# Making the tables of further tiles four steps earlier in two expert layers, and loading expert 29's down weights into X instead of ROW

## The chip, the cores and the metric

The kernel runs on one core of one Trainium2 chip. The metric is the device time of one execution in microseconds (us), as the median of several runs. The five engines are TensorE (PE, with PEld for its weight loads), VectorE (DVE), ScalarE (ACT), GpSimd (POOL) and SyncE (SP). SP computes nothing here: it only issues transfers, in program order, each behind the waits that its buffer needs.

## The reference

Two transformer blocks over 256 tokens of width 1024 in float32. Block one has latent attention beside a long convolution, cross attention and a mixture of 32 experts; then comes a root-mean-square norm. Block two has a recurrent layer beside block attention, and again 32 experts. What matters here is the expert layer, and the norm between the blocks:

```python
for g in range(N_GROUPS):                       # block one: 4 groups of 8 experts
    a = jnp.einsum('td,edf->tef', t, w_gate[g])
    b = jnp.einsum('td,edf->tef', t, w_up[g])
    m = jax.nn.silu(a) * b * combine[:, g, :, None]
    y = y + jnp.einsum('tef,efd->td', m, w_down[g])
...
return _rms(x, final_norm_g)                    # between the blocks
...
hdn = jax.nn.silu(jnp.einsum('td,edf->tef', xc, w1)) * jnp.einsum('td,edf->tef', xc, w3)
return jnp.einsum('tef,efd->td', hdn * gate[:, :, None].astype(hdn.dtype), w2)   # block two
```

`combine` and `gate` are zero but for two experts of each token.

## The kernel before

**Experts.** `moe(b)` handles block b (1 or 2) on each engine. The 512 pairs of token and expert are sorted by expert, and each expert has one *tile* of slots: 32 slots in block one, 64 in block two. The layer is a row of 32 *steps*, one for each expert. In step e TensorE does gate and up of expert e (L1253 in block one, L1248 in block two), adds the rows of expert e-2 to the tokens (L1296), and does the down product of expert e-1 (L1268). VectorE in its step e does `hidden(e-1)`, `x_window(e+1)`, `to_slots(e-1)` and `low_part(e-1)`; the last one ends in L2829 and L2835 in block two.

**Further tiles.** An expert with more pairs than slots needs further tiles, which are run after the 32 steps. Their number, start, expert and rank come from tables on one partition, which VectorE makes piece by piece inside four of its steps: `extra_counts`, `extra_slots`, `extra_starts`, `extra_experts`. The last one writes the results as integers to `tabi` and raises the semaphore `routed`. The variable `looped` fixes the four steps: they are `looped - 4` to `looped - 1`, which is 12 to 15 in block one and 8 to 11 in block two. Steps below `looped` are written out, and those from `looped` to 27 run in a hardware loop. In block one the tables lie in the tile X, in block two in XN. In block two `order_of_steps`, at step 2, also writes the order in which experts 8 to 30 are taken.

**Weights.** Each expert has 2 MB of gate and up weights and 1 MB of down weights. SP issues them as two transfers. Block one has six places for them: four in `ring`, and two beside it, whose down halves are the tiles ROW and HT (`apart`). Expert 6's down weights go to X once. `in_six` refills a place as soon as `gu_done1` or `down_done1` say that its last user is through; the down weights of expert e wait for expert e-6's down product. Expert 29's go to ROW. Block two has the four places of `ring`, and one outside for expert 4. There expert e's weights wait for expert e-4's products (from expert 9 on). Experts 5 to 11 are issued by written-out code (L704, L706). Then SP waits until `routed` is 3 (L708), which is what `extra_experts` of block two raises it to, and issues experts 12 to 31 in a loop (L714, L716).

**Between the blocks.** ROW also takes `final_norm_g`, spread over all partitions by a transfer of 0.5 MB that POOL issues (L3352) when `down_done1` says that 30 down products are through. `gained` on VectorE (L3050, L3052) needs it. From it follow the norm of block two, TensorE's transposes of it (L783), the products `ada(10)` and `ada(11)` with two 2 MB pieces of `w_ada` (L924), and the input projection `xl` (from L798). `ada11` can be issued only when the last down product of block one has freed its place.

Of the kernel before, what the change touches and what calls it, by code (L numbers as in the profile page):

```python
# [46 lines left out]
NE = G * EPG  # L47
# [8 lines left out]
RING = 4  # L56
SLOT = 3 * KD * FE
# [114 lines left out]
SIX = RING + 2  # L172
# [3 lines left out]

GU = 2 * KD * FE
FEAT = S + 2 * FFN


STAGES = [("f1", 1, (1,)), ("hT", 4, (6, 7, 2, 4)), ("lat", 2, (3, 0)), ("f2", 1, (5,)), ("f3_0", 4, (1, 6, 7, 2)),
# [90 lines left out]
def two_blocks(nc, A, out):  # L272

    ctx = ExitStack()
    with ctx:
# [5 lines left out]
        def sem(name):  # L281
            if name not in made:
                made[name] = ctx.enter_context(nc.semaphore(name))
            return made[name]
# [4 lines left out]
        X = sb("X", [P, TT, D])  # L289
# [303 lines left out]
        def _(sp):  # L593
# [4 lines left out]
            def in_six(w):  # L598

                base = MOE_AT[0]  # L600

                def refill_gate(e, q, src):

                    s = slot(base + q)
                    sp.wait_ge(sem("gu_done1"), e - (SIX - 1))
                    if q < RING:
                        sp.dma_start(ring[:, s, 0:GU], src[:, 0:GU]).then_inc(sem(f"slot_full{s}"), 16)
                    else:
                        sp.dma_start(apart[q - RING][0], src[:, 0:GU]).then_inc(sem(f"beside_gu{q - RING}"), 16)

                def refill_down(e, q, src, places=SIX):

                    sp.wait_ge(sem("down_done1"), e - (places - 1))
                    if q < RING:
                        sp.dma_start(ring[:, slot(base + q), GU:SLOT], src[:, GU:SLOT]).then_inc(sem(f"slot_down{q}"), 16)
                    else:
                        sp.dma_start(apart[q - RING][1], src[:, GU:SLOT]).then_inc(sem(f"beside_d{q - RING}"), 16)

                refill_gate(SIX, 0, w[SIX, :, :])
                for e in range(SIX + 1, 2 * SIX + 1):  # L620
                    refill_gate(e, e % SIX, w[e, :, :])
                    refill_down(e, (e - 1) % SIX, w[e, :, :], SIX + 1)
                with sp.Fori(2 * SIX + 1, NE - 2 * SIX, SIX) as e0:
                    for q in range(SIX):
                        src = w[bass.ds(e0 + q, 1)].rearrange("a p f -> p (a f)")
                        refill_gate(e0 + q, (q + 1) % SIX, src)
                        refill_down(e0 + q, q, src)
                for e in range(NE - SIX - 1, NE - 1):
                    refill_gate(e, e % SIX, w[e, :, :])
                    if e == NE - 2:  # L630
                        refill_gate(NE - 1, (NE - 1) % SIX, w[NE - 1, :, :])
                    refill_down(e, (e - 1) % SIX, w[e, :, :])
                refill_down(NE - 1, (NE - 2) % SIX, w[NE - 1, :, :])

            def half_outside(w, q):
# [97 lines left out]

            at = dict(UNITS)["filt"] - FEAT
            for t in range(TT):
                sp.dma_start(X[:, t, :], A["x"][t * P:(t + 1) * P, :]).then_inc(sem(f"x_in{t}"), 16)
            sp.dma_start(tab[:, 0:P], A["tab"][:, 0:P]).then_inc(sem("tab"), 16)
            sp.dma_start(col[:, :], A["col"]).then_inc(sem("tab"), 16)
            sp.dma_start(ring[:, slot(0), at:at + FEAT], A["filt"][:, at:at + FEAT]).then_inc(sem("feat"), 16)
            load(PLACE["lat"], A["lat"], dict(UNITS)["lat"])  # L740
# [10 lines left out]
            n = experts(0)  # L751
# [14 lines left out]
        def _(pe):  # L766
# [202 lines left out]
            w = arrived(pe, "mla")  # L969
# [141 lines left out]
            def moe(b):  # L1111
# [8 lines left out]
                for k in range(KD):  # L1120
                    ready(pe, f"rT{b}", k // 2)
                    g = 64 * (k % 2)
                    n = min(64, KD * (G + NE) - k * (G + NE))
# [186 lines left out]
                    return (r - ways) % RING if in_turn(e) else r  # L1310

                uses_1 = [-(-(NE - q) // SIX) for q in range(SIX)]
                downs_1 = [-(-(NE - 1 - q) // SIX) for q in range(SIX)]

                def gate_of_six(n, r):

# [7 lines left out]

                def down_of_six(n, r):

                    if r == SIX and isinstance(n, int):
                        pe.wait_ge(sem("down_in_x"), 16)
                        return X[:, :, :].rearrange("p t d -> p (t d)")
                    if r > SIX or not isinstance(n, int):  # L1330
                        r = r - 1
                    q, use = r % SIX, r // SIX
                    if q >= RING:
                        pe.wait_ge(sem(f"beside_d{q - RING}"), n * 16 + 16 * (use + 1))
                        return apart[q - RING][1]
                    pe.wait_ge(sem(f"slot_down{q}"), n * 16 + 16 * (use + 1))
                    return ring[:, slot(base + q), GU:SLOT]
# [111 lines left out]
                looped = NE - RING  # L1449
# [19 lines left out]
                n = pe.value_load(tabi[0:1, XCOUNT[b]:XCOUNT[b] + 1], min_val=0, max_val=NX[b] - 1)  # L1469
# [4 lines left out]
                with pe.If(n > 0):  # L1474
                    with pe.Fori(0, n) as j:
                        w = ring[:, slot(base + 4 - 2 * b), :]
# [727 lines left out]
        def _(dve):  # L2204
# [367 lines left out]
            for h in range(XH):  # L2572
                ready(dve, f"xs{h}")
                link(V.reciprocal(xinv[:, h, :], xsum[:, h, :]))
                for t in range(TT):
                    p = prob[:, h % 2, t, :]
# [37 lines left out]
            def moe(b):  # L2614
# [241 lines left out]
                r = slice(0, 1)  # L2856
                c1, s1, x1, xi1, xe1 = counts[r, :], starts[r, :], nx[r, :], xincl[r, :], xex[r, :]
                mk, tm, mb = mk8[b][r], tm8[b][r], mk8b[b][r]
                n = NX[b]
# [67 lines left out]
                if b == 1:  # L2927
# [5 lines left out]
                    dve.wait_ge(sem("silu1"), 2)  # L2933
                    dve.wait_ge(sem("down_done1"), 1)
                    times_up(hb).then_inc(sem("hb1"), 1)
                looped = (5 - b) * RING
                for e in range(3 - b, looped):
                    if b == 1 and e == 2:
                        x_window(3, 1)
# [385 lines left out]
        def _(pool):  # L3325
# [56 lines left out]
            pool.dma_start(relb[0:BUCKETS, :], A["rel_bias_2"]).then_inc(sem("onehot"), 16)  # L3382
            G_.memset(relb[BUCKETS:BUCKETS + 1, :], NEG).then_inc(sem("mask_row"), 1)
            pool.wait_ge(sem("mask_row"), 1)
            pool.wait_ge(sem("down_done1"), SIX * (NE // SIX))
            broadcast_row(ROW[:, 0:1024], "final_norm_g", D, "rows")
            pool.wait_ge(sem("f_gain"), 2 * TT)
            pool.dma_start(ROW[:, 0:1024], A["gates_w"]).then_inc(sem("gates_w"), 16)
# [99 lines left out]
```

## Time and profile before

| | us |
|---|---|
| median of 3 runs | 922.76 |
| the runs | 922.76, 1696.45, 921.23 |
| profiled execution, device time | 919.3 |
| its span, first to last instruction | 917.4 |
| TensorE busy in it | 857.7 |
| VectorE busy in it | 532.2 |
| ScalarE busy in it | 362.2 |

The 1696.45 stands alone and belongs to a disturbed run. The profiled execution took 919.3, of which 917.4 is the span and 1.9 lies around it; all times of rows count from the start of the span. Block one's steps lie between about 306 and 505 us, block two's between about 665 and 904 us. The whole span moved 285.39 MB at a mean of 311 GB/s, and its chain of waits is put down to TensorE for 62%, to transfers for 17% and to VectorE for 12%. A busy share is an average over stages with different limits, so the rows of one stage say more than these.

### The profile page before, as it was taken

To read this page: it belongs to the slowest core of one execution; us is meant where nothing else is said; L and a number is where in the kernel's file an instruction comes from. 1 tells how busy PE (TensorE), PEld (TensorE's weight loads), DVE (VectorE), ACT (ScalarE), POOL (GpSimd) and SP (SyncE) were. 2 spreads that over 40 slices of the span, in tenths; PEclk is the share of its full clock that TensorE was granted. 3 is DMA by queue.
4 is the path that set the end of the run, shared out by engine and by line. 5 is a ranking of instruction groups with operands and counts; after the bars stand their busy time and mean duration, and the time that the engine had idled before them with its cause. 6 is when DMAs were issued, how large, how long until landed. Compare 5 with 4: busy or idle time off the path is not lost.

```text
span 917.4 us, 15466 instructions
## 1 busy us (share of the span) xinstructions
PE 857.7 (93%) x5774; PEld 543.9 (59%) x5774; DVE 532.2 (58%) x1182; ACT 362.2 (39%) x711; POOL 22.3 (2%) x41
## 2 busy tenths in 40 slices
PE   8999999999999899989998799999899979999995
PEld 6778558888976333433433499766654535555552
DVE  5877668465455645675554775988843543333335
ACT  5574435455354333323332657645421111111113
POOL 1010111000000000000000000000000000000000
PEclk9999999999999999999999999999999989999998
DMA  9655895547647899999999985613789849999991
GB/s 353 252 192 222 321 386 201 186 167 270 265 165 309 345 411 424 424 425 427 424 426 420 422 315 200 233 44 121 292 304 384 321 196 429 425 422 424 426 420 50
DMA packets 28904, 285.39 MB, mean 311 GB/s; under 512 B 3080, under 2 KB 5544, under 8 KB 7856
## 3 DMA queue, kind: packets, MB, share of 16 engines
q1 hardware_dynamic: 25344, 278.25, 75.1%
q0 software_dynamic: 1136, 3.74, 1.2%
q10 hardware_dynamic: 2368, 2.64, 0.9%
q8 instruction: 36, 0.59, 0.3%
q14 instruction: 20, 0.16, 0.0%
HBM read 283.56 MB, written 1.06 MB: 310 GB/s over the span
## 4 chain that ended last, share of the span: by engine, by line
PE 62%; DMA 17%; DVE 12%; ACT 4%; issue 3%; SPq 1%; DVEq 1%; ACTq 0%
DMA ring<-in_experts 14%; PE bank L798 8%; PE bank L1248 7%; PE bank L800 7%; PE bank L799 7%; PE bank L1268 6%; PE bank L1253 4%; PE bank L1296 4%; PE bank L1219 3%; DVE ring_r L535 2%; PE bank L1260 2%; DMA ring<-in_ada 2%; PE bank L924 1%; PE bank L1225 1%; DMA ring<-in_lat 1%
## 5 line engine op out<-in xcount | busy, mean ns | idle before, releaser
L535 DVE TENSOR_TENSOR ring_r<-ring,ring_r 128x1024 fp32r<-128x1024 f32 (+1 forms) x84 | 99.4, 1213 | 66.8 <-ACT ring_r L528 66.7
L1248 PE MATMUL bank<-ring,arena 128*64 128x256 f32 x992 | 115.7, 386 | 12.8 <-DMA ring<-in_experts 12.2
L528 ACT ACTIVATE ring_r<-ring 128x1024 fp32r<-128x1024 f32 (+1 forms) x84 | 85.0, 1046 | 68.5 <-PE bank L800 67.6
L798 PE MATMUL bank<-HT_r,ring_r 128*128 128x256 f32 x352 | 101.9, 289 | 1.3 <-DVE arena_r L2269 0.7
L1248 PEld LDWEIGHTS bank<-ring,arena 128*64 128x64 f32 x992 | 75.0, 138 | 45.9 <-issue 13.2
L800 PE MATMUL bank<-HT_r,ring_r 128*128 128x256 f32 x352 | 99.6, 283 | 0.0
L1268 PE MATMUL bank<-ring,arena 128*64 128x512 f32 (+1 forms) x416 | 81.7, 600 | 1.6 <-DMA ring<-in_experts 1.0
L799 PE MATMUL bank<-XN_r,ring_r 128*128 128x256 f32 x288 | 81.5, 283 | 0.0
L2829 DVE SCALAR_TENSOR_TENSOR arena<-bank,arena 128x512 f32<-128x512 f32 x32 | 24.0, 750 | 99.0 <-PE bank L1268 99.0
L1962 ACT ACTIVATE arena<-bank 128x512 f32<-128x512 f32 (+1 forms) x64 | 31.4, 491 | 117.5 <-PE bank L1248 94.8
L1296 PE MATMUL bank<-arena_r 64*128 64x512 f32 x496 | 74.2, 417 | 2.9 <-DVE arena_r L2836 2.4
L798 PEld LDWEIGHTS bank<-HT_r,ring_r 128*128 128x128 f32 x352 | 67.4, 192 | 4.5 <-issue 4.3
L1296 PEld LDWEIGHTS bank<-arena_r 64*128 64x128 f32 x496 | 41.8, 184 | 47.1 <-issue 33.3
L800 PEld LDWEIGHTS bank<-HT_r,ring_r 128*128 128x128 f32 x352 | 67.5, 192 | 0.0
L1977 ACT ACTIVATE arena_r<-arena 128x512 fp32r<-128x512 f32 x31 | 19.5, 630 | 103.7 <-DVE arena L2829 103.7
L799 PEld LDWEIGHTS bank<-XN_r,ring_r 128*128 128x128 f32 x288 | 55.2, 192 | 1.0 <-issue 1.0
L2836 DVE SCALAR_TENSOR_TENSOR arena_r<-bank,arena,arena_r 128x512 fp32r<-128x512 f32 x31 | 23.3, 751 | 51.6 <-ACT arena_r L1976 51.6
L1260 PEld LDWEIGHTS bank<-tab,arena 128*128 128x128 f32 x192 | 19.9, 140 | 51.0 <-issue 50.3
L1253 PE MATMUL bank<-ring,arena 128*32 128x512 f32 x352 | 42.3, 598 | 4.4 <-DMA ring<-in_experts 2.1
L1268 PEld LDWEIGHTS bank<-ring,arena 128*64 128x64 f32 (+1 forms) x416 | 20.4, 125 | 43.2 <-issue 40.3
L798 PE MATMUL bank<-ring_r,HT_r 128*128 128x512 f32 (+1 forms) x96 | 37.6, 391 | 1.7 <-DVE ring_r L535 1.3
L800 PE MATMUL bank<-ring_r,arena_r 128*128 128x512 f32 x96 | 37.6, 391 | 0.0
(509 smaller groups left out, 1439.1 us busy)
## 6 DMA issues: line engine op xcount, KB each, us to landing
ring<-in_experts SPq DMA_DIRECT2D x53, 2048.0 KB, 19.1
ring<-in_experts SPq DMA_DIRECT2D x52, 1024.0 KB, 16.5
ring<-in_ada SPq DMA_DIRECT2D x12, 2048.0 KB, 11.5
arena<-in_experts SPq DMA_DIRECT2D x10, 2048.0 KB, 17.8
ring<-in_win SPq DMA_DIRECT2D x5, 2048.0 KB, 14.9
ring<-in_hy SPq DMA_DIRECT2D x3, 2048.0 KB, 17.2
HT<-in_experts SPq DMA_DIRECT2D x6, 1024.0 KB, 15.2
ROW<-in_experts SPq DMA_DIRECT2D x5, 1024.0 KB, 15.7
```

Of the source, the lines that this page charges most:

```text
L528: nc.scalar.activation(R(h), w, ACT.Copy).then_inc(sem("w_high"), 1)
L535: nc.vector.tensor_tensor(R(w), w, R(h), ALU.subtract).then_inc(sem("w_low"), 1)
L798: mm(ps, R(ah), R(bh), start=first, stop=False)
L799: mm(ps, R(ah), R(bl), start=False, stop=False)
L800: return mm(ps, R(al), R(bh), start=False, stop=last_)
L1219: last = mm(list_bank[g:g + wide, :], picked[:, i, t, :], XN[:, t, h * 512:(h + 1) * 512], start=True, stop=True)
L1248: last = mm(gu_bank[g * wide:(g + 1) * wide, 0:256], xw[:, k, :], w[k // 4][:, k % 4, g * 256:(g + 1) * 256], start=k == 0, stop=k == KD - 1)
L1253: last = mm(gu_bank[g:g + wide, :], xw[:, 2 * (k % 4) + k // 4, :], w[k // 4][:, k % 4, :], start=k < sides, stop=k >= KD - sides)
L1260: last = tr(guT_bank[:, c * P:(c + 1) * P], gu_sb[:, c * P:(c + 1) * P], ident)
L1268: last = mm(d_bank[g:g + wide, :], hb[:, f, :], w[:, o:o + 512], start=b == 1 or f == 0, stop=b == 1 or f == 1)
L1296: last = mm(acc[2 * t + h][:, :], R(onto[b][rows, i, t * P:(t + 1) * P]), R(u[rows, :]), start=False, stop=False)
L1962: A_(gu_sb[:, 0:gu_cols], gu_bank[:, 0:gu_cols], ACT.Copy).then_inc(sem(f"gu_sb{b}"), 1)
```

## The change

`looped` is 4 lower for both blocks. Block one's tables are made in steps 8 to 11, block two's in steps 4 to 7, and VectorE's hardware loops begin at 12 and 8. Expert 29's down weights go to X, behind two waits: `routed` at 1 (block one's tables, which lie in X, are finished) and `down_done1` at 7 (expert 6's down weights, which lie there too, are used). With that ROW's last user is expert 23, and POOL may issue the `final_norm_g` transfer when `down_done1` is 24. The rest counts the semaphores anew. No instruction is added or dropped in what is executed.

```diff
+DOWN_IN_X = (SIX, NE - 3)
...
-                    refill_down(e, (e - 1) % SIX, w[e, :, :])
+                    if e == DOWN_IN_X[1]:
+                        sp.wait_ge(sem("routed"), 1)
+                        sp.wait_ge(sem("down_done1"), SIX + 1)
+                        sp.dma_start(X[:, :, :].rearrange("p t d -> p (t d)"), w[e, :, GU:SLOT]).then_inc(sem("down_in_x"), 16)
+                    else:
+                        refill_down(e, (e - 1) % SIX, w[e, :, :])
...
-                downs_1 = [-(-(NE - 1 - q) // SIX) for q in range(SIX)]
+                downs_1 = [-(-(NE - 1 - q) // SIX) - (q == (DOWN_IN_X[1] - 1) % SIX) for q in range(SIX)]
...
-                    if r == SIX and isinstance(n, int):
-                        pe.wait_ge(sem("down_in_x"), 16)
+                    if isinstance(n, int) and r in DOWN_IN_X:
+                        pe.wait_ge(sem("down_in_x"), 16 * DOWN_IN_X.index(r) + 16)
                         return X[:, :, :].rearrange("p t d -> p (t d)")
...
-                looped = (5 - b) * RING
+                looped = (4 - b) * RING
...
-            pool.wait_ge(sem("down_done1"), SIX * (NE // SIX))
+            pool.wait_ge(sem("down_done1"), DOWN_IN_X[1] - SIX + 1)
             broadcast_row(ROW[:, 0:1024], "final_norm_g", D, "rows")
```

On VectorE, at step 7 of block two, before the change (from `hidden(6)` to `to_slots(6)`; `waits` names the semaphores, and TENSOR_LOAD reads a number of `tabi`):

```order
L2775 TENSOR_TENSOR arena<-arena,bank 128x128 [waits down_done2,silu2]
L2611 TENSOR_LOAD tabi
L2611 ISA x2
L2815 ISA [waits gu_done2]
L2815 COPY arena<-arena 128x512
L2822 COPY arena<-arena 128x2 [waits to_tokens2]
L2825 TENSOR_SCALAR arena_r<-tab,arena 128x256 [waits cur2]
```

The same place after the change (line numbers are 6 higher here):

```order
L2821 COPY arena<-arena 128x512
L2925 TENSOR_TENSOR XN<-XN,tab 1x256
L2926 TENSOR_REDUCE XN<-XN 1x8 [waits dve_step]
L2927 CAST tabi<-XN 1x8 [waits dve_step]
L2928 CAST tabi<-XN 1x8
L2929 CAST tabi<-XN 1x8
L2930 CAST tabi<-arena 1x1
L2960 TENSOR_LOAD tabi [waits routed]
L2960 ISA x2
L2962 TENSOR_LOAD tabi
L2962 ISA x2
```

The last piece of block two's tables, with the CAST that raises `routed`, stood at step 11 and stands at step 7 now, between the copy of the next expert's tokens and `to_slots(6)`.

On SP, at expert 29 of block one, before:

```order
L609 DMA arena<-in_experts 128x4096 [waits gu_done1]
L617 DMA ROW<-in_experts 128x2048 [waits down_done1]
L607 DMA ring<-in_experts 128x4096 [waits gu_done1] x2
L617 DMA HT<-in_experts 128x2048 [waits down_done1]
L615 DMA ring<-in_experts 128x2048 [waits down_done1]
```

and after:

```order
L610 DMA arena<-in_experts 128x4096 [waits gu_done1]
L636 DMA X<-in_experts 128x2048 [waits down_done1,routed]
L608 DMA ring<-in_experts 128x4096 [waits gu_done1] x2
L618 DMA HT<-in_experts 128x2048 [waits down_done1]
L616 DMA ring<-in_experts 128x2048 [waits down_done1]
```

The transfer keeps its place in SP's order; its destination and the counts that it waits for are others.

## Rows read from the trace of the kernel before

**Rows 1.** The profile's page: the span.
```profile
span 917.4 us, 15466 instructions
```
**Rows 2.** Waits of SP's queue: us in total, times, longest.
```profile
SPq L708 <- DVE tabi L2924: 17.5, 1, 17.5
```
**Rows 3.** Timeline of SP, block two: start, us, line, transfer.
```profile
725.61 0.33 SPq L706 DMA_DIRECT2D ring<-in_experts  x1
744.80 0.34 SPq L714 DMA_DIRECT2D ring<-in_experts  x1
```
**Rows 4.** Windows: window, length, busy per engine, PEclk, DMA share, GB/s.
```profile
730.00:740.00 10.00, 10.00 (x70) 4.61 (x68) 6.40 (x19) 1.18 (x3) 0.00 (x0) 1.00 0.16 64
```
**Rows 5.** Timeline of PE, block two: gates 9, 11, 12, 17, 28, 30, 31.
```profile
725.73 3.67 PE L1248 MATMUL bank<-ring,arena 128*64 128x256 f32 x32
...
739.66 3.67 PE L1248 MATMUL bank<-ring,arena 128*64 128x256 f32 x32
...
752.35 5.50 PE L1248 MATMUL bank<-ring,arena 128*64 128x256 f32 x32 [5.64 <-DMA ring<-in_experts]
...
789.43 3.67 PE L1248 MATMUL bank<-ring,arena 128*64 128x256 f32 x32 [0.34 <-DMA ring<-in_experts]
...
870.79 3.67 PE L1248 MATMUL bank<-ring,arena 128*64 128x256 f32 x32 [0.35 <-DMA ring<-in_experts]
...
887.14 3.67 PE L1248 MATMUL bank<-ring,arena 128*64 128x256 f32 x32 [1.40 <-DMA ring<-in_experts]
...
894.94 3.67 PE L1248 MATMUL bank<-ring,arena 128*64 128x256 f32 x32
```
**Rows 6.** Timeline of DVE, step 11 of block two: start, us, then idle before.
```profile
743.28 0.13 DVE L2924 CAST tabi<-arena 1x1 int32<-1x1 f32 x1
...
748.35 0.69 DVE L2835 TENSOR_TENSOR arena_r<-arena,arena_r 128x512 fp32r<-128x512 f32 x1 [0.69 <-ACT arena_r L1977]
```
**Rows 7.** Transfers issued between 725 and 726: KB, us to landing.
```profile
ring<-in_experts SPq DMA_DIRECT2D x1, 1024.0 KB, 7.1
```
**Rows 8.** Timeline of PE, block one: gates 12, 13 and 17.
```profile
379.63 1.92 PE L1253 MATMUL bank<-ring,arena 128*32 128x512 f32 x16
385.49 1.92 PE L1253 MATMUL bank<-ring,arena 128*32 128x512 f32 x16
...
413.56 1.92 PE L1253 MATMUL bank<-arena 128*32 128x512 f32 x16
```
**Rows 9.** Windows, block one.
```profile
360.00:420.00 60.00, 55.78 (x460) 22.54 (x456) 39.79 (x100) 20.21 (x38) 0.00 (x0) 1.00 1.01 424
```
**Rows 10.** Windows over the four stretches of table work, block one, then two.
```profile
sum 11.24, PE 11.24 PEld 4.58 DVE 9.85 ACT 2.39 POOL 0.00; mean PE 2.81 PEld 1.14 DVE 2.46 ACT 0.60 POOL 0.00
...
sum 10.66, PE 10.66 PEld 5.24 DVE 7.83 ACT 1.16 POOL 0.00; mean PE 2.67 PEld 1.31 DVE 1.96 ACT 0.29 POOL 0.00
```
**Rows 11.** Transfers issued at 360 to 363, then at 743 to 745.
```profile
ring<-in_experts SPq DMA_DIRECT2D x1, 2048.0 KB, 13.5
...
ring<-in_experts SPq DMA_DIRECT2D x1, 2048.0 KB, 7.5
```
**Rows 12.** The profile's page: the transfer of the norm's scale.
```profile
ROW<-in_final_norm_g POOLq DMA_DIRECT2D x1, 512.0 KB, 11.9
```
**Rows 13.** Timeline of POOL.
```profile
498.91 0.58 POOL L3352 DMA_DIRECT2D ROW<-in_final_norm_g  x1 [231.75 <-PE bank L1268]
```
**Rows 14.** Timeline of DVE after block one's experts.
```profile
510.87 0.69 DVE L3052 SCALAR_TENSOR_TENSOR X<-bank,ROW 128x512 f32<-128x512 f32 x1 [3.02 <-DMA ROW<-in_final_norm_g]
```
**Rows 15.** Timeline of PE, last down product, `ada(10)`, `ada(11)`.
```profile
505.13 1.07 PE L1268 MATMUL bank<-ring,arena 128*32 128x512 f32 x8 [0.96 <-DMA ring<-in_experts]
...
514.13 3.40 PE L924 MATMUL bank<-ring,cm 128*32 128x512 f32 x16 [3.56 <-DVE st L3059]
...
521.08 1.92 PE L924 MATMUL bank<-ring,cm 128*32 128x512 f32 x16 [1.65 <-DMA ring<-in_ada]
```
**Rows 16.** Windows: the clock as TensorE starts `ada(10)`.
```profile
514.00:514.50 0.50, 0.37 (x4) 0.23 (x8) 0.48 (x2) 0.50 (x1) 0.28 (x1) 0.50 1.16 492
```

## The prediction, made before the changed kernel had run

> **What bounds the kernel now.** I read the page first, then SP's waits, since SP's queue feeds every weight, and then block two stage by stage. The profiled execution took 919.3 us: its span of 917.4 [rows 1] and 1.9 around it.
>
> The list of SP's waits has one line that is not the usual wait for a free place: 17.5 us at L708, once, for a cast of VectorE's [rows 2]. In SP's timeline nothing is issued between 725.61 and 744.80 [rows 3]. In the windows the transfers move 64 GB/s from 730 to 740 [rows 4], against 424 in a loaded stretch [rows 9]. VectorE's timeline has the cast at 743.28, the end of the tables in step 11 [rows 6]. So the weight stream of block two stands still because the tables are late, not for want of a place.
>
> What that costs is seen on TensorE. Up to step 11 its steps last 6.965 us, half of 725.73 to 739.66, with no wait. At 752.35 it has idled 5.64 us for gate 12's weights, and the 32 products take 5.50 us instead of 3.67, since the clock fell while it waited. From gate 17 at 789.43 to gate 28 at 870.79 eleven steps last 7.396 us each, with some 0.35 us of waiting in each: that is the pace of the stream, 3 MB per expert. All of [rows 5]. The stall therefore costs three times: the wait, the slow clock, and a stream that runs level with TensorE for the rest of the layer.
>
> **The change part by part.**
>
> *Block two, steps 4 to 7.* TensorE's step is 6.965 us at steps 9 to 11 [rows 5], where the tables are made now, so they cost it nothing there, and steps 4 to 7 hold the same other work. Of step 11, the worst, VectorE's last operation L2835 starts at 748.35 and ends at 749.04 [rows 6]; what TensorE needs it for comes behind its next gate and would, without the stall, begin at 739.66 + 6.965 + 3.6 = 750.2 (a gate takes 3.67) [rows 5]. So 1.2 us is left, and I price the move at 0. If that cover were gone, up to 10.66 us of table work [rows 10] would show. `routed` now reaches 3 about 4 x 6.965 = 27.9 us before 743.28, at 715.4, while SP comes to L708 at about 726: the 17.5 us go entirely.
>
> What is late next? The last transfer before the stall, expert 11's down weights, was issued at 725.61 and landed 7.1 us later, at 732.7 [rows 3, 7]. With the next one queued behind it, gate 12 lands two thirds of a stream step later: 732.7 + 4.9 = 737.6. TensorE wants it at 739.66 + 6.965 = 746.6, so 9.0 us are in hand. The stream needs 7.396 per expert and TensorE 6.965, so 0.43 is lost per step, and 8.2 of the 9.0 by gate 31. Near the end of the present run two steps were longer by 1.6 us together than the stream's pace: 887.14 - 870.79 = 16.35 for two steps, against 14.79 [rows 5]. With these the stock is used up at gate 30 or 31. I take a wait of 0.3 there; its bounds are 0 and 2.
>
> So from gate 9 to gate 31 there are 22 steps of 6.965, 153.2 us, and one list product before the last gate: 894.94 - 887.14 - 6.965 = 0.8. That is 154.1, against 894.94 - 725.73 = 169.2 now [rows 5]. The gain is 15.1, less 0.3: **14.8 us**. What follows gate 31 has the same work.
>
> *Block one, steps 8 to 11.* Here the tables do delay TensorE: four steps from gate 13 to gate 17 last 28.07 us, against 4 x 5.86 = 23.44, so 4.6 us are lost [rows 8]. They move to about gates 9 to 13. But the transfers are saturated there (share 1.01, 424 GB/s [rows 9]), and the end of the layer waits for weights [rows 15]. The delay would matter only if the queue ran dry. A gate transfer issued at about 362 lands after 13.5 us, one that finds the queue empty after 7.5 [rows 11], so 6.0 us are queued, more than 4.6. The slowed steps also last on average 7.0 us, about the stream's 7.4, so the queue keeps its length. Cost 0; bounds 0 and 4.6.
>
> *Expert 29's down weights in X.* The transfer keeps its place in SP's order; both new waits were met long before. Behind it stand gates 30 and 31, which wait for their own places. The queue is full, so an earlier issue lands no earlier. Cost 0, and no gain.
>
> *The norm's scale, 0.5 MB.* POOL issues it at 498.91 now, and it lands 11.9 us later, at 510.8 [rows 12, 13]; `gained` idles 3.02 us until 510.87 [rows 14]. After the change it is issued when 24 down products are through, in step 24, whose gate starts near 413.56 + 7 x 5.86 = 454.6 [rows 8], and lands well before it is wanted. VectorE can then start up to 3.0 us sooner; TensorE's last products after 505.13 take part of that, and I take **1.7 us**, with 0.7 and 3.0 as bounds. But its bytes now pass ahead of all of the last weights. By the row, with 11.9 us in flight and 505.13 as the time when TensorE takes the last down weights [rows 15], about half of the 0.5 MB had passed by then; the other half is 0.7 us at 424 GB/s, by which the last down product is later. The Trainium skill ("DMA: Bandwidth & Descriptors", section on queues, rings and completion order) says that each of the 16 engines takes turns between the queues packet by packet; by that, all the bytes would have passed after some 2.5 us, and the 0.7 would be 0. The row speaks against equal turns.
>
> Does the 1.7 us reach the path? TensorE's `ada(11)` waited for its weights at 521.08, not for VectorE [rows 15]. They sit in a saturated queue, and the bytes ahead of them are the same. The 2 MB cannot be sooner; two other transfers that follow `gained` (the gates' weights, the bias rows) start 1.7 us sooner and take a share of the queue, which I estimate at **0.5 us later** for `ada11`. Bounds: 0 and 1.2, the whole 0.5 MB at 424 GB/s.
>
> *The clock.* TensorE's pause before `ada(10)` was 3.56 us, and the clock was at 0.50, 1.2 GHz, when it started again; the 16 products took 3.40 us. Its pause before `ada(11)` was 1.65 us, and the same products took 1.92 [rows 15, 16]. After the change the first pause shrinks by 1.7, to about 1.9. The transposes end near 519.43 - 1.7 = 517.7, and the second pause grows to 521.5 - 517.7 = 3.8 us. That is nearest to the 3.56 that lost the clock. The fall moves from a place off the path to one on it: 1.5 us on `ada(11)`, and a little on the projection behind it, **1.7 us** together. Bounds: 0 (no fall), and 1.83, what gate 12 lost [rows 5].
>
> Sum: -14.8 + 0 + 0.5 + 1.7 = -12.6. Against the profiled 919.3 that is 906.7. The undisturbed timed runs, 922.76 and 921.23, have a mean of 922.0, 2.7 above it; there I expect **909.4 us**. Against the median shown, 922.76, 2% is 18.5 us, so this is a change within 2%. (About 2% is what a measurement of this kernel can tell from no change.)
>
> **The rivals.**
>
> *A. The clock does not fall at `ada(11)`.* For it: between 1.65 and 3.56 no row tells where the fall begins, and if VectorE gains less than 1.7 the pause is shorter. Against it: the estimate of 3.8 lies above a pause that lost it. Gain 14.3: 907.7.
>
> *B. TensorE meets the stream well before the end.* If the stream holds 7.5 us per expert in place of 7.396, or the last transfer before the stall lands 2 us later, the 9.0 us in hand are gone by about gate 27, and the last four or five steps go at the stream's pace, with the 1.6 us of the last two. For it: the margin at the end is near 0. Against it: eleven steps at 7.396. The gain is smaller by 3: 912.4.
>
> *C. Another wait takes the flag's place, and the stream stands still as before.* SP would have to find a place not free at 727. Expert 12's place was free when gate 8 was through, at 725.73 - 6.965 + 3.67 = 722.4 [rows 5], and the queue drained only at 732.7. So nothing in the profile speaks for it. It gives 922.0 + 2.2 = 924.2.
>
> *D. The tables have no cover where they go (the slower side).* In block one, VectorE sets the pace at steps 10 to 13, and all 11.24 us of table work show instead of 4.6; 6.0 of them are absorbed by the queue, and 5.2 reach the stream. In block two all 10.66 show at steps 4 to 7 [rows 10]. Sum: -14.8 + 5.2 + 10.7 + 2.2 = +3.3, or 925.3. It decides from 12.6 us of table work that reach the path. Against it stand the 6.965 us steps at 9 to 11 and the 4.6 of block one.
>
> *E. The earlier norm gets through.* If `ada11` lands about 1.7 us sooner because less is in the queue at 506, its term turns from +0.5 to -1.7 and the pause stays short, so the clock holds: gain 14.8 + 1.7 = 16.5, 905.5.
>
> **How the numbers follow.** Forecast 0.50, A 0.19, B 0.15, C 0.04, D 0.03, E 0.09. The likeliest is the forecast, 909.4. The range reaches down to A and to E less the 1.5 us by which the profiled run may be nearer to what a run shows: 904. It reaches up to B with 1.2 for the whole 0.5 MB and 1.5 of the 4.6 us of block one: 915. It leaves out C, D and the tails, under 2 in 10. Faster by over 2% means below 904.3: the low tails of A and E, and of the forecast if the timing favours it, 0.17. Slower by over 2% would need 941 and is the far tail of C and D, 0.02. Within 2%: 0.81.
>
> **What would show it.** In the changed kernel's profile: no wait of SP at L714 (the old L708) on VectorE's cast, and a stream share near 1 from 715 on; steps of 6.965 us in block two from 3 to about 29, with no idle time before gate 12 and a full clock; gate 31 some 154 us behind gate 9. In block one steps 10 to 13 longer by 4.6 in all, and transfers still near 424 GB/s. Between the blocks VectorE's L3058 without a wait for ROW, `ada(10)` in 1.92 us, `ada(11)` after a pause of nearly 4 us in 3.4. Wrong would be: gates 20 to 31 waiting for weights with 7.4 us steps (B), steps 4 to 8 of block two above 7 us (D), or the last down product of block one above 507.

## The result, and the profile after

Four runs of the changed kernel gave a median of 907.89 us (906.67 to 911.46), where the forecast was 909.4 and its range 904 to 915. Four runs of the kernel before on the same chip have a median of 922.0 us. The ratio is 0.9859, with a 95% interval from 0.9821 to 0.9898: faster by 1.0 to 1.8%. Single disturbed runs, 1696.45 here and 2149.16 in e3 below, are left out of the ratios but not of the medians. The profiled execution took 906.67 us, where the forecast, counted against the profiled execution of before, said 906.7. Line numbers of the new kernel are 6 higher from SP's loops on (L1248 is L1254 now).

The page of the changed kernel: the span, the busy times, and the shares of the chain that ended last.

```profile
span 904.8 us, 15502 instructions
PE 857.0 (95%) x5774; PEld 538.6 (60%) x5774; DVE 533.1 (59%) x1182; ACT 362.1 (40%) x711; POOL 22.2 (2%) x41
PE 75%; DVE 11%; DMA 7%; ACT 4%; issue 2%; DVEq 0%; SPq 0%; ACTq 0%
```

TensorE is busy 95% of the span, and the transfers have only 7% of the chain. The page counts 36 instructions more than before, so it is not quite true that none was added; the counts of the engines' busy instructions are the same, so the 36 are of the kinds that are not counted as busy (registers, branches, semaphores).

SP's timeline in block two (start, us, line, transfer), to be read against [rows 3]:

```profile
728.11 0.33 SPq L712 DMA_DIRECT2D ring<-in_experts  x1
729.85 0.34 SPq L720 DMA_DIRECT2D ring<-in_experts  x1
```

Two issues that were 19.19 us apart are 1.74 apart. The wait for the flag [rows 2] has no line any more: the cast that raises it now starts at 717.82. The windows (window, length, busy time per engine, PEclk, DMA share, GB/s) have no hole either; the first row here answers to [rows 9], the second covers what was the hole of [rows 4]:

```profile
360.00:420.00 60.00, 56.65 (x456) 22.49 (x452) 39.64 (x96) 20.15 (x38) 0.00 (x0) 0.97 1.01 424
725.00:755.00 30.00, 30.00 (x214) 15.25 (x216) 10.87 (x26) 5.05 (x13) 0.00 (x0) 1.00 1.01 424
```

TensorE's timeline in block two, gates 9, 12, 30 and 31, against [rows 5]:

```profile
728.19 3.67 PE L1254 MATMUL bank<-ring,arena 128*64 128x256 f32 x32
...
749.09 3.67 PE L1254 MATMUL bank<-ring,arena 128*64 128x256 f32 x32
...
874.49 3.67 PE L1254 MATMUL bank<-ring,arena 128*64 128x256 f32 x32
...
882.29 3.67 PE L1254 MATMUL bank<-ring,arena 128*64 128x256 f32 x32
```

No gate has idle time in front of it. Gate 9 to gate 31 takes 882.29 - 728.19 = 154.10 us, against 169.21 before: 15.1 us gained. But gate 9 itself is 728.19 - 725.73 = 2.5 us later, and that was lost between the blocks. TensorE's, VectorE's and POOL's timelines there (last column: idle before, and what ended it), against [rows 13 to 15]:

```profile
505.35 1.06 PE L1274 MATMUL bank<-ring,arena 128*32 128x512 f32 x8 [0.35 <-DVE arena L2780]
...
512.23 1.92 PE L930 MATMUL bank<-ring,cm 128*32 128x512 f32 x16 [1.26 <-DVE st L3065]
...
521.07 3.64 PE L930 MATMUL bank<-ring,cm 128*32 128x512 f32 x16 [4.01 <-DMA ring<-in_ada]
```
```profile
508.97 0.69 DVE L3058 SCALAR_TENSOR_TENSOR X<-bank,ROW 128x512 f32<-128x512 f32 x1 [0.71 <-PE bank L1293]
```
```profile
460.19 0.58 POOL L3358 DMA_DIRECT2D ROW<-in_final_norm_g  x1 [193.47 <-PE bank L1274]
```

The scale is there in time, VectorE starts 1.90 us sooner, and `ada(10)` runs in 1.92 us where it took 3.40. All of this is off the path: `ada(11)` starts at 521.07, as it did at 521.08, because its weights decide. Now it is `ada(11)` that starts on a slow clock. The windows show it:

```profile
525.00:526.00 1.00, 1.00 (x6) 1.00 (x6) 0.00 (x0) 0.37 (x1) 0.00 (x0) 0.50 0.98 406
526.00:527.00 1.00, 1.00 (x9) 1.00 (x8) 0.00 (x0) 0.00 (x0) 0.00 (x0) 0.75 1.05 437
527.00:528.00 1.00, 1.00 (x11) 1.00 (x10) 0.00 (x0) 0.00 (x0) 0.00 (x0) 1.00 1.00 417
```

The granted clock is 0.50, 1.2 GHz, until after 526, over the 16 products and a part of the projection behind them. The first product behind that projection is the one of line L1520 (L1514 in the kernel before); its start, before and after:

```profile
546.94 3.62 PE L1514 MATMUL bank<-arena,ROW 128*128 128x256 f32 x16
```
```profile
549.46 3.62 PE L1520 MATMUL bank<-arena,ROW 128*128 128x256 f32 x16
```

From the start of `ada(11)` it comes after 28.39 us, where it came after 25.86. That is the 2.5 us.

In block one, TensorE's timeline of gates 9 to 12 and the product at which the clock falls, against [rows 8]:

```profile
361.60 1.92 PE L1259 MATMUL bank<-ring,arena 128*32 128x512 f32 x16
367.45 1.92 PE L1259 MATMUL bank<-arena 128*32 128x512 f32 x16
374.92 1.92 PE L1259 MATMUL bank<-arena 128*32 128x512 f32 x16
...
379.90 1.93 PE L1225 MATMUL bank<-XN,arena 128*32 128x512 f32 x8 [0.56 <-DVE arena L2631]
...
384.36 1.92 PE L1259 MATMUL bank<-ring,arena 128*32 128x512 f32 x16
```

Steps 10 and 11 last 7.47 and 9.44 us instead of 5.86, a loss of 5.2. The stream stays at 424 GB/s (first windows row above), and the last down product starts at 505.35 against 505.13: the loss does not reach the end of the block.

### The profile page after: what moved, and what is told of

Same layout as the page of the kernel before. It is cut to its first block, busy times and chain, and to the rows that moved or that the text cites. A ratio compares the mean times of both kernels' runs of the same rounds, so it can differ in the third digit from the quotient of the medians.

```text
span 904.8 us, 15502 instructions
## 1 busy us (share of the span) xinstructions
PE 857.0 (95%) x5774; PEld 538.6 (60%) x5774; DVE 533.1 (59%) x1182; ACT 362.1 (40%) x711; POOL 22.2 (2%) x41
## 4 chain that ended last, share of the span: by engine, by line
PE 75%; DVE 11%; DMA 7%; ACT 4%; issue 2%; DVEq 0%; SPq 0%; ACTq 0%
PE bank L1254 13%; PE bank L1274 9%; PE bank L804 8%; PE bank L806 7%; PE bank L805 7%; PE bank L1302 6%; PE bank L1259 5%; DMA ring<-in_experts 4%; PE bank L1225 3%; PE bank L1266 3%; DVE ring_r L536 2%; PE bank L930 2%; DMA ring<-in_ada 2%; PE bank L1231 1%; DMA ring<-in_lat 1%
## 5 line engine op out<-in xcount | busy, mean ns | idle before, releaser
L1254 PE MATMUL bank<-ring,arena 128*64 128x256 f32 x992 | 113.9, 382 | 0.6 <-DVE arena L2758 0.6
L1254 PEld LDWEIGHTS bank<-ring,arena 128*64 128x64 f32 x992 | 68.9, 137 | 36.9 <-issue 5.9
L1919 ACT ACTIVATE arena<-bank 128x512 f32<-128x512 f32 x32 | 19.1, 597 | 47.2 <-PE bank L1225 47.2
```

The lines of the kernel that those rows point to most:

```text
L1254: last = mm(gu_bank[g * wide:(g + 1) * wide, 0:256], xw[:, k, :], w[k // 4][:, k % 4, g * 256:(g + 1) * 256], start=k == 0, stop=k == KD - 1)
```

## The experiments

Each was timed beside the kernel before on its own chip (that kernel's medians: 922.0 us for the change, 920.77 to 920.82 for the experiments). A profiled execution's time is its span and 1.9 us.

| kernel | median us | ratio and 95% interval | span us | gates 9 to 31 of block two, us |
|---|---|---|---|---|
| the change | 907.89 | 0.9859 [0.9821, 0.9898] | 904.8 | 154.10 |
| e1 tables only | 906.19 | 0.9833 [0.9810, 0.9857] | 904.5 | 154.10 |
| e2 long fill | 907.14 | 0.9852 [0.9830, 0.9875] | 904.5 | 154.10 |
| e3 transfers only | 923.8 | 1.0030 [1.0015, 1.0045] | 922.0 | 169.07 |
| e4 no wait for the flag | 905.85 | 0.9835 [0.9813, 0.9857] | 902.7 | 154.10 |
| e5 short fill | 906.73 | 0.9847 [0.9830, 0.9865] | 903.2 | 154.11 |
| e6 held for 11 gates | 914.2 | 0.9930 [0.9910, 0.9950] | 911.7 | 162.23 |
| e7 held for 12 gates | 921.3 | 1.0006 [0.9994, 1.0018] | 917.4 | 169.26 |
| e8 block two's tables only | 907.3 | 0.9856 [0.9834, 0.9878] | 905.4 | 154.53 |
| e9 held for 10 gates | 906.64 | 0.9855 [0.9834, 0.9877] | 907.8 | 155.98 |
| e10 no wait, two fills | 905.67 | 0.9833 [0.9820, 0.9846] | 905.1 | 155.09 |
| e11 the change, two fills | 906.73 | 0.9849 [0.9835, 0.9862] | 904.5 | 154.39 |

The theory at this point: the whole gain is SP's wait for the flag, and the transfers' part costs some time, by the clock, between the blocks. Rivals: the tables' new place has a worth or a price of its own; the moved transfers bring a part of the gain.

### One part at a time: e1, e3

```diff
 # e1: the kernel before, with
-                looped = (5 - b) * RING
+                looped = (4 - b) * RING
 # e3: the changed kernel, with
-                looped = (4 - b) * RING
+                looped = (5 - b) * RING
```

> The change without its part on ROW and X: only the steps of the tables move, in both blocks. Theory (the tables' flag gives 15.1 us in block two; the early norm scale costs 2.5 by the clock that falls before ada(11)): the 2.5 come back, span near 917.4 - 15.1 = 902.3, ratio to the kernel before 0.984; ada(11) takes 1.9 us after a pause under 2. Rival (the 2.5 between the blocks come from block one's tables in steps 8 to 11): span stays near 904.8, ratio 0.986.

> Only the part on ROW and X, with the tables where they were. Theory: VectorE's gained starts some 2 us sooner, ada(11) no sooner, the clock falls: slower by 2.5, span 919.9, ratio 1.003. Rival (an earlier norm is a gain by itself that the full change hides): span 915.7 or less, ratio 0.998.

The tables alone give the whole gain; that e1 is below the change (0.9833 against 0.9859) the intervals do not separate. The transfers alone make the kernel slower by 0.15 to 0.45%, or 1.4 to 4.1 us. `ada(11)` in the profile of e1, then of e3:

```profile
523.21 1.92 PE L924 MATMUL bank<-ring,cm 128*32 128x512 f32 x16 [1.06 <-DMA ring<-in_ada]
```
```profile
523.15 3.64 PE L930 MATMUL bank<-ring,cm 128*32 128x512 f32 x16 [3.97 <-DMA ring<-in_ada]
```

It starts at the same time in both; only with the transfers' part does it start on the slow clock. From there to the first product of L1514 (L1520) it is 25.87 us in e1 and 28.48 in e3. So the 2.5 us belong to that part of the change.

The spans, 904.5 and 922.0, were each some 2 us above what was expected, and e1's is the number of its rival; the ratios, and `ada(11)` itself, were as the theory had them. Both profiles hold something else, which fills that gap. Block one's last down product is at 507.25 and 507.47, over 2 us later than in the kernel before. It begins at the block's first gate, where the clock falls. Windows of e1, then of the changed kernel:

```profile
306.00:310.00 4.00, 4.00 (x25) 1.08 (x18) 2.15 (x11) 0.63 (x3) 0.00 (x0) 0.59 0.42 111
```
```profile
306.00:310.00 4.00, 3.66 (x32) 1.45 (x24) 3.01 (x13) 1.59 (x4) 0.00 (x0) 1.00 0.60 172
```

As I read it, the slow start delays SP's refills (111 GB/s against 172), and the stream that sets the end of the block keeps the delay. From the first gate to the last down product it is 201.8 and 201.4 us in these two, and 198.2 to 199.8 in the other profiles. This scatter of some 2 us is in no kernel's favour, and the profiled spans have to be read with it.

### The wait alone: e4

```diff
 # the kernel before, without the wait ahead of SP's loop over experts 12 to 31
-                sp.wait_ge(sem("routed"), 3)
```

> The kernel before, with the tables in steps 12 to 15 and 8 to 11 as they were, but SP does not wait for routed at 3 ahead of its loop over experts 12 to 31 of block two (it still does ahead of the further tiles, which alone read those tables). Theory (only the flag held the stream): the whole gain of block two without moving any table, 15.1 us, span 902.3, ratio 0.984, gate 9 to gate 31 in 154.1 us. Rival (the table work itself in steps 8 to 11 holds something up, or SP meets another wait at 727): at most half of it, span 910 or more.

The edit is safe: the order of the experts that the loop reads from `tabi` is written at step 2 and guarded by `routed` at 2, and the tables that `routed` at 3 announces are read only for the further tiles, behind a wait of their own. No table is moved and the time is that of e1. SP's timeline, then gates 9 and 31:

```profile
725.97 0.33 SPq L706 DMA_DIRECT2D ring<-in_experts  x1
727.72 0.34 SPq L713 DMA_DIRECT2D ring<-in_experts  x1
```
```profile
726.09 3.67 PE L1247 MATMUL bank<-ring,arena 128*64 128x256 f32 x32
...
880.19 3.67 PE L1247 MATMUL bank<-ring,arena 128*64 128x256 f32 x32
```

154.10 us, to the hundredth what the change gives. The tables were never too late for anything but this one wait.

### How much of a hold is lost: e6, e7, e9

If the wait is the cause, putting it back by degrees must give the time back by degrees. All three are e1 with a wait ahead of SP's loop until 11, 12 or 10 gates are through. Gates count from 0, so these are gates 10, 11 and 9: the gate numbers in the three expectations are one too high, and the loop's first transfer does bring gate 12's weights, which e7's expectation denies.

```diff
+                sp.wait_ge(sem("gu_done2"), 11)      # e7: 12, e9: 10
```

> Early tables alone (no transfer changed), and the sync engine's loop of the second block is held until gate 11's products are done (one wait ahead of its first issue), so that expert 12's gate weights are asked for about 740 us instead of 730. Theory (the 17.5 us hold ahead of that loop is the whole loss of the kernel before, and a shorter hold is absorbed in part by the slack of the ring): the issue moves about 12 us, the transfer of 7.1 us lands about 748, a microsecond or so before gate 12; that gate waits 0 to 1 us and the later ones in the loop 6 to 8 us together, so about half of the gain stays: ratio 0.988 to 0.993. Rival (the hold counts only by what gate 12 waits): ratio 0.983 to 0.985. Rival (any hold costs the whole): 0.998 to 1.001.

> As the run before, held until gate 12's products are done would be one step later than the weights that the loop's first issue brings can allow: gate 12's own weights of the ring are issued ahead of the loop, the first of the loop is for a later expert. Theory: the issue comes at about 752 us, as late as or later than the 745 of the kernel before, so all of the 15 us is lost and some more: ratio 0.999 to 1.008. Rival (the tables beside steps 8 to 11 cost something themselves in the kernel before, beside the flag): ratio 0.990 to 0.997 although the issue is as late.

> Early tables alone, the sync engine's loop of the second block held until gate 10's products are done, so that its first issue comes at about 732.5 us (held at gate 11 it came at 739.01 and the 22 steps took 162.23 us, 8.1 more than without a hold). Theory (the stream of weights is the second limit of this loop: with a hold each later step takes 7.39 us, the stream's pace, so every microsecond of hold is lost but for about 1 us of slack; held at gate 11, a hold of some 9 us lost 8.1): a hold of about 2.5 us loses 1 to 2 us, no wait at gates 12 to 20, short ones of 0.3 to 0.45 us from some gate behind 20 on; 22 steps in 155 to 156.3 us, ratio 0.985 to 0.987. Rival (a hold costs only where the weights of the next gates come late): 154.1 us, ratio 0.983 to 0.985.

SP's timeline of e6, then of e7, then of e9, the last issue before the hold and the first behind it:

```profile
726.78 0.33 SPq L706 DMA_DIRECT2D ring<-in_experts  x1
739.01 0.34 SPq L715 DMA_DIRECT2D ring<-in_experts  x1
```
```profile
725.53 0.33 SPq L706 DMA_DIRECT2D ring<-in_experts  x1
744.73 0.34 SPq L715 DMA_DIRECT2D ring<-in_experts  x1
```
```profile
729.13 0.33 SPq L706 DMA_DIRECT2D ring<-in_experts  x1
734.40 0.34 SPq L715 DMA_DIRECT2D ring<-in_experts  x1
```

A hold is the distance of the two, less the 1.74 us that it is without one:

| kernel | hold us | gates 9 to 31 us | lost against 154.10 | hold less loss |
|---|---|---|---|---|
| e9 | 3.5 | 155.98 | 1.9 | 1.6 |
| e6 | 10.5 | 162.23 | 8.1 | 2.4 |
| e7 | 17.5 | 169.26 | 15.2 | 2.3 |
| before | 17.5 | 169.21 | 15.1 | 2.4 |

Every microsecond of hold is lost but for about two. Those two are not slack of TensorE's. When SP stops, transfers are still in flight, so the stream runs on for a while. What it stood is read from the bytes moved in the 24 us from gate 9 on; before, e7, e6, e9, and the changed kernel (last column GB/s):

```profile
725.73:749.73 24.00, 20.98 (x151) 10.71 (x150) 15.74 (x47) 4.34 (x11) 0.00 (x0) 0.99 0.41 161
```
```profile
725.65:749.65 24.00, 20.97 (x151) 10.71 (x150) 9.58 (x22) 4.33 (x11) 0.00 (x0) 0.99 0.42 167
```
```profile
726.90:750.90 24.00, 24.00 (x181) 12.79 (x182) 9.58 (x22) 4.34 (x11) 0.00 (x0) 1.00 0.72 290
```
```profile
729.25:753.25 24.00, 24.00 (x181) 12.79 (x182) 9.59 (x22) 4.35 (x11) 0.00 (x0) 1.00 0.99 409
```
```profile
728.19:752.19 24.00, 24.00 (x181) 12.79 (x182) 9.59 (x22) 4.33 (x11) 0.00 (x0) 1.00 1.01 425
```

Against 425 GB/s that is 14.9, 14.6, 7.6 and 0.9 us of standing, and 15.1, 15.2, 8.1 and 1.9 us were lost. So all of the stream's standing time is lost, and 0.2 to 1.0 us more, which is no more than the kernels without a hold differ by (154.10 to 155.09).

e6 shows how the loss comes about. Its gates 9, 12, 14, 15, 30 and 31:

```profile
726.90 3.67 PE L1249 MATMUL bank<-ring,arena 128*64 128x256 f32 x32
...
747.80 3.67 PE L1249 MATMUL bank<-ring,arena 128*64 128x256 f32 x32
...
762.08 3.67 PE L1249 MATMUL bank<-ring,arena 128*64 128x256 f32 x32 [0.28 <-DMA ring<-in_experts]
769.47 3.67 PE L1249 MATMUL bank<-ring,arena 128*64 128x256 f32 x32 [0.35 <-DMA ring<-in_experts]
...
881.33 3.67 PE L1249 MATMUL bank<-ring,arena 128*64 128x256 f32 x32 [1.27 <-DMA ring<-in_experts]
889.13 3.67 PE L1249 MATMUL bank<-ring,arena 128*64 128x256 f32 x32
```

Gate 12, whose weights the hold delayed, does not wait at all. The loss comes later, in small pieces: from gate 14 on TensorE waits a third of a microsecond in each step, and the steps last 7.39 us. e7 waits at gate 12 as the kernel before did, and loses the clock there:

```profile
752.31 5.39 PE L1249 MATMUL bank<-ring,arena 128*64 128x256 f32 x32 [5.69 <-DMA ring<-in_experts]
...
894.91 3.67 PE L1249 MATMUL bank<-ring,arena 128*64 128x256 f32 x32
```

The slow clock of e7 is no extra loss: it loses no more per microsecond of standing than e6, which has neither that wait nor the fall. The stream sets the end of the layer in all of them, and what TensorE loses on the way is time that it would have waited. In e9 the waits begin only near the end; its gate at 855.23 is the first of four:

```profile
855.23 3.67 PE L1249 MATMUL bank<-ring,arena 128*64 128x256 f32 x32 [0.35 <-DMA ring<-in_experts]
...
885.23 3.67 PE L1249 MATMUL bank<-ring,arena 128*64 128x256 f32 x32
```

Of the expectations, e6's and e9's theory was met in the number of the 22 steps and in where the waits stand (e6's 8.1 us is a tenth above its "6 to 8"). e9's ratio alone could not have told it from its rival: the interval from 0.9834 to 0.9877 holds both. e7's was met in the ratio, 1.0006, but its issue came at 744.73 and not at about 752. So e7 did not test a longer hold. It repeats the hold of the kernel before, 17.5 us, with the tables early, and takes the same 169.3 us: where the tables are made is worth nothing beside the hold.

### Whose tables: e8

```diff
 # the kernel before, with
-                looped = (5 - b) * RING
+                looped = (5 - b) * RING if b == 1 else (4 - b) * RING
```

> The kernel before with the tables four steps earlier in block two alone; block one and the transfers are as before. Theory (block one's earlier tables cost TensorE about 5 us there, but the saturated stream of weights sets that block's end, so they cost nothing): same as both blocks' tables moved, ratio 0.983 to 0.985. Rival (block one's tables delay the stream through later issues): this one is faster than both moved by 1 to 2 us, ratio 0.981 to 0.982.

The ratio, 0.9856, is inside e1's interval and missed the range named for the theory by 0.0006; it is also above the rival's. So leaving block one's tables in their place gains nothing that can be seen. In the profile, the scale of the norm happened to land after 10.6 us instead of 11.9, VectorE waited only 0.91 us for it, and `ada(11)` lost the clock as in the changed kernel, though no transfer was changed:

```profile
512.27 1.92 PE L924 MATMUL bank<-ring,cm 128*32 128x512 f32 x16 [1.46 <-DVE st L3059]
...
521.57 3.44 PE L924 MATMUL bank<-ring,cm 128*32 128x512 f32 x16 [4.47 <-DMA ring<-in_ada]
```

From there to L1514 it is 27.52 us, 1.7 more than in the kernel before. In a kernel whose transfers are not changed, the scale's landing decides in each execution how long each of the two pauses is. In e4 neither lost the clock, after 3.23 and 2.32 us; in before, e1, e6, e7, e9 and e10 the first did, after 3.44 to 3.98 us. With the transfers' part the first pause was 1.25 or 1.26 us in all five profiles, and the second, where nothing filled it, 3.97 or 4.01.

### Filling the pauses: e2, e5, e10, e11

```diff
 # e2 and e5: the changed kernel; e2 with 15, e5 with 8
             transposed("uT", XN, KD, "xn_u")
+            occupy("xl", 0, 15)
             ada(11)
 # e10: e4, e11: the changed kernel; occupy("xl", 0, 5) at that place, and in first_steps
                     token_rows(0).then_inc(sem("gathered"), 1)
+                    busy(2)
                     gather_T(0)
+                    busy(4)
 # busy(n) is n products of ident and 256 columns of iota into the gate's bank
```

> The whole change, and 15 matmuls of 128x256 (some 3.7 us) that write a bank nobody reads yet, between the transposes and ada(11), where TensorE waits 4.0 us for weights. Theory (only the clock costs there): ada(11) starts at 521.1 as before, takes 1.9 instead of 3.6 us, and the span falls by 2.5 to 902.3, ratio 0.984. Rival (the early norm scale costs by its bytes or by the order of the transfers): ada(11) is no earlier and the matmuls give nothing, or they delay it; span 904.8 or more.

> The changed kernel with 8 filling matmuls between the transposes after the first block and the last of the modulation's column products; the 15 of the earlier fill ran 6.6 us in all (with the 8 transposes beside them) and pushed that product from 521.07 to 523.27 us. Theory (the 1.72 us that the product takes longer, 3.64 instead of 1.92, and the slow columns after it come from the clock, which fell in the idle 4.01 us): the fill ends before the transfer lands, the product starts at about 521.1 and runs 1.92 us, the next transposes' landmark follows 25.9 us after it instead of 28.4, profiled span about 902.3, ratio to the kernel before 0.983 to 0.984 against the change's 0.986. Rival (the slow product comes with the data, not with the clock): 3.6 us again, span 904.8. Rival (the pause is refilled but the time is given back in a later wait): product 1.92 us, span still 904 or more.

> The kernel before without the sync engine's wait for the flag ahead of its loop of the second block (that version: 905.85 us, span 902.7), and TensorE filled in two pauses: 2 and 4 matmuls of 256 columns before the first block's first gate (idle 0.71 and 1.29 us there; in two of the profiles so far the clock fell at this gate and the block ended 2.1 to 2.3 us later), and 5 before the last of the modulation's column products (fell there in three profiles, 1.5 to 1.7 us). Theory (both losses are the clock's): the first gate in 1.92 us in every execution, block one's end near 505, that product in 1.92 us, times of 903.5 to 905.5 us, ratio 0.981 to 0.983, below every version so far. Rival (the fill delays the first gate as much as it saves, or block one's end moves by other things): 905 to 907, ratio 0.983 to 0.985.

> The change with the same two fills. Theory (the change differs from the kernel without the flag's wait only in where the clock falls between the blocks): same time as that one with fills within 1 us, span 902.5 to 903.5, ratio 0.981 to 0.983. Rival (block one's earlier tables or the transfer into X cost something of their own): 1 us or more above the other, ratio 0.984 to 0.986.

e2's fill was too long: `ada(11)` kept the clock, and L1521 followed it by 25.87 us, but it began only at 523.27, so nothing was gained. e5, the fill (each of its products is two records) and `ada(11)`:

```profile
516.44 3.62 PE L781 MATMUL bank<-tab 128*128 128x256 f32 x16
521.91 1.92 PE L930 MATMUL bank<-ring,cm 128*32 128x512 f32 x16 [1.85 <-DMA ring<-in_ada]
```

With the pause filled the products take 1.92 us and L1521 follows 25.88 us after them, as in the kernel before. This shows that the 2.5 us between `ada(11)` and that product are the clock's. The weights landed 0.8 us later in this execution (15.8 us after their issue, 14.6 in the changed kernel's profile), so the span fell by 1.6 and not by 2.5, and the ratio, 0.9847, missed the 0.983 to 0.984 expected and cannot be told from the change's.

e10 and e11 had `ada(11)` and block one's first gate in 1.92 us too, but that gate came about 0.5 us later behind the fills, and block one ended at 506.06 and 506.78: no sooner than without. Their times, 905.67 and 906.73, are those of the rivals. That a fill at block one's first gate is worth anything is not shown. e11's rival, that the change has a price of its own beside the clock, stays open: with both pauses filled its median is 1.1 us above e10's, and e2, e5 and e11 (0.9847 to 0.9852) all lie above e1, e4 and e10 (0.9833 to 0.9835), but the intervals overlap. The lowest times of all are those of e4 and e10, the kernel before without one wait; against the change (0.9859) they are lower by 0.25%, which the intervals do not separate.

## Why the prediction was right

- **Block two, -14.8: measured -15.1.** The stop of the stream and what it cost were as argued. The 22 steps and the list product took 154.10 us, the figure in the text. The wait of 0.3 at gate 30 or 31 was 0 in the changed kernel, e4 and e5; in e8, e11 and e10, where nothing holds SP either, the 22 steps took 0.4, 0.3 and 1.0 us more, with waits for weights at the last gates (e10's were 0.49 and 0.36). The "9.0 us in hand" can be read directly: SP issued expert 12's gate weights at 729.85, they landed 10.8 us later, at 740.65, and gate 12 began at 749.09, so 8.4 were in hand. With 8.2 used up, TensorE and the stream come to the end almost together, and that is why the holds found no slack. Rival B's place was right and its price too high; by its own figures, too, the stock lasts to gate 28 or 29, not 27.
- **The view of the stall as costing three times.** The sum was right; the account of it wasn't quite. The runs with a hold show one cost, the time for which the stream stood, and all of it is lost. The wait at gate 12 and its slow clock lie inside that, not beside it.
- **Tables in block two, 0:** right, and e4 shows it from the other side, since the same 154.10 us come with the tables where they were.
- **Block one, 0 on the path, 4.6 on TensorE:** 5.2 on TensorE, of which 0.6 is a fall of the clock that the text did not foresee (e1 and e5, with the tables in the same steps and no fall, lost 4.6 over steps 10 to 12), and 0.2 at the end of the block. The steps that grew were 10 and 11, not 10 to 13. Counted from the block's first gate the last down product is 0.7 later (199.76 against 199.09), which is inside the scatter above. That the queue hides it is shown by the stream's 424 GB/s and by e8, which is not faster than e1.
- **The transfer into X, 0:** nothing in the profile of the changed kernel waits for it, but it was not run apart from the scale's.
- **The norm's scale, 1.7 us sooner and off the path:** 1.9 us sooner, off the path. The last down product was 0.2 later, not 0.7 (the text's own working gives 0.6: 0.48 of 1.24 us).
- **`ada(11)` lands 0.5 later:** 0.0 in the changed kernel's profile. In all profiles the transfer took 14.5 to 16.2 us, so a half microsecond can be neither shown nor excluded.
- **The clock, +1.7: measured +2.5.** The mechanism was right to the pause (3.8 forecast, 4.01 found), and e3 and e5 show it alone. The size was short, because the bound was read from gate 12, where 32 products of 3.67 us lost 1.83. Here the clock stayed at 0.50 until 526.5, past `ada(11)` and into the dense projection behind it. The bound should have been the whole stretch at the slow clock, 5.4 us of work of which half is lost, not one group of products. The size also differs from one profile to the next: 2.5 here, 2.6 in e3, 1.7 in e8 after a longer pause (4.47).

The errors cancel: 0.3 and 0.5 to the good, 0.8 to the bad. That the sum met the profiled time to the tenth is in part luck, since block one's first gate alone scatters by 2 us. C, D and E did not occur: SP finds its place free, block two's steps 4 to 7 are covered, and `ada(11)` was not sooner.

## What to carry to other kernels

When transfers run at their ceiling, ask how long their queue stands empty, not which gate waits: here each microsecond in which the stream stood still was a microsecond of the kernel, though in e6 the gate whose weights were late had none to wait. Ask also whether the wait in a queue's instructions guards what stands behind it; here it did not, and taking it away gave what a rearrangement of the work behind the flag gave. And where an engine has two pauses in a row, the second ended by something that does not move, shortening the first lengthens the second, and a slow clock can move with it onto the path.

## What the runs showed of the hardware

- The stream holds 424 GB/s over stretches of 30 and 60 us, with a DMA share of 1.01. The Trainium skill ("DMA: Bandwidth & Descriptors", section on where the 436 GB/s come from) has 425 GB/s for a transfer of 16 MB, which this agrees with, and says in the same place that about 358 bind what comes from HBM. Just above, it says that its own figures are for one core with its neighbour idle. With one core at work the rows here do not show the limit of 358.
- The clock fell to 0.50 not only after single pauses of 3.4 to 5.7 us. In e1 and e3 it fell at block one's first gate, where TensorE had idled 0.71 and 1.29 us between short groups of products, and in the changed kernel near 380, where the idle time just before was 0.56 us. In the other profiles without a fill there the first gate kept the full clock, and so did the place near 380 in four of the eight profiles with the tables there (e1, e5, e9, e11). The Trainium skill ("TensorE: Matmul & The Clock Gate", section on psum-queue depth-cycling) tells of another kernel in which small idle times between groups of matmuls come often enough for the clock to go back and forth. The rows agree in that short pauses were enough, and show that at one and the same place of the code it differs from one execution to the next.
- The same 0.5 MB transfer of POOL, issued into the saturated stream, took 10.6 us (e8) to 12.1 us (the changed kernel) to land in the thirteen profiles, where its bytes alone are 1.2 us at 424 GB/s. That spread was enough for the slow clock to strike one group of products in the kernel before and another in e8.
